# Joint attention with split f32r scores, halved value sums and split keys and queries in place

## The reference

```python
SEQ, CTX, A_HEADS, A_NOPE, A_ROPE, A_V, A_QK = 512, 256, 8, 64, 32, 64, 96
def _attend(q, k, v):
    s = jnp.einsum('bqhd,bkhd->bhqk', q, k).astype(jnp.float32) * (A_QK ** -0.5)
    p = jax.nn.softmax(s, axis=-1).astype(v.dtype)
    return jnp.einsum('bhqk,bkhd->bqhd', p, v)
for l in range(DEPTH):                       # two layers
    fy, gy, qy, ky, vy, ay = _branches(hy, *params, None)      # context, 256 tokens
    fx, gx, qx, kx, vx, ax = _branches(hx, *params, rope)      # sequence, 512 tokens
    ox = _blocked_attention(qx, concat(ky, kx), concat(vy, vx)) * silu(ax)
    x = x + gate * (concat([fx, gx, ox]) @ w_out[l])
    if l < DEPTH - 1:                        # layer 0 alone updates the context
        oy = _attend(qy, ky, vy) * silu(ay)
        y = y + gate_c * (concat([fy, gy, oy]) @ w_out[l])
```

## Time and profile before

| | before |
|---|---|
| median of three runs | 2172.76 us (2172.22 to 2173.36) |
| profiled execution | 2174.57 us, of which the span is 2173.2 us |
| PE busy | 2145.1 us, 99% |
| PE's weight loads | 1754.2 us, 81% |
| VectorE busy | 997.2 us, 46% |
| ScalarE busy | 799.3 us, 37% |
| GpSimd busy | 734.5 us, 34% |
| line 2729, scores | 288 matmuls, 114.6 us |
| line 2741, transposes | 416 matmuls, 60.0 us |
| line 2761, values | 832 matmuls, 87.6 us |

### The profile page before, as it was taken

How to read it: one execution, slowest core, us unless ns; L and a number is a source line. 1 busy time by engine, 2 the same in 40 slices (tenths; PEclk the granted TensorE clock), 3 DMA queues, 4 the chain that set the end, 5 groups by cost and what they waited for, 6 DMA issues and landing times.

```text
span 2173.2 us, 30673 instructions
## 1 busy us (share of the span) xinstructions
PE 2145.1 (99%) x12586; PEld 1754.2 (81%) x12586; DVE 997.2 (46%) x1764; ACT 799.3 (37%) x1371; POOL 734.5 (34%) x339
## 2 busy tenths in 40 slices
PE   9999999999999999999999999999999999999999
PEld 8778888888889898888878888887886667886677
DVE  5664555541222333334465555345305673552672
ACT  6445333333333333334443333333225442334531
POOL 3116444455443333333174444443221002232102
PEclk9999999999999999999999999999999999999999
DMA  4103444432322222221034444322110001322002
GB/s 153 40 30 110 145 145 146 144 126 97 107 93 88 82 81 82 78 88 69 35 121 146 145 146 146 135 97 95 59 68 35 1 1 40 110 78 83 1 2 78
DMA packets 57659, 191.53 MB, mean 88 GB/s; under 512 B 8112, under 2 KB 11440, under 8 KB 57264
## 3 DMA queue, kind: packets, MB, share of 16 engines
q1 hardware_dynamic: 46128, 155.82, 20.6%
q10 hardware_dynamic: 11392, 33.75, 4.4%
HBM read 185.35 MB, written 2.10 MB: 86 GB/s over the span
## 4 chain that ended last, share of the span: by engine, by line
PE 88%; DVE 3%; ACT 1%; issue 1%; DVEq 1%; POOL 0%; ACTq 0%; POOLq 0%; DMA 0%
PE ps L180 21%; PE ps L181 21%; PE ps L182 21%; PE ps L2729 4%; PE ps L183 3%; PE ps L185 3%; PE ps L184 3%; PE ps L2761 2%; PE ps L2741 2%; PE ps L1105 2%; PE ps L1139 1%; PE ps L1121 1%; PE ps L2284 0%; PE ps L2250 0%; PE ps L2097 0%
## 5 line engine op out<-in xcount | busy, mean ns | idle before, releaser
L253 POOL TENSOR_TENSOR w_lo<-w_raw,w_hi 128x1024 fp32r<-128x1024 f32 x282 | 682.0, 2419 | 1332.2 <-ACT w_hi L170 1318.0
L170 ACT ACTIVATE w_hi<-w_raw 128x1024 fp32r<-128x1024 f32 x284 | 300.3, 1058 | 539.3 <-DMA w_raw<-in_wstream 539.0
L180 PE MATMUL ps<-h_hi,w_hi 128*128 128x512 f32 x1168 | 464.0, 397 | 2.7 <-DVE w_lo L295 1.8
L182 PE MATMUL ps<-h_hi,w_lo 128*128 128x512 f32 x1168 | 455.0, 390 | 0.0
L181 PE MATMUL ps<-h_lo,w_hi 128*128 128x512 f32 x1168 | 455.0, 390 | 0.0
L180 PEld LDWEIGHTS ps<-h_hi,w_hi 128*128 128x128 f32 x1168 | 219.3, 188 | 50.7 <-DVE w_lo L295 2.0
L182 PEld LDWEIGHTS ps<-h_hi,w_lo 128*128 128x128 f32 x1168 | 219.3, 188 | 46.0
L181 PEld LDWEIGHTS ps<-h_lo,w_hi 128*128 128x128 f32 x1168 | 219.5, 188 | 43.3 <-issue 0.7
L183 PE MATMUL ps<-w_hi,h_hi 128*128 128x256 f32 x416 | 116.6, 280 | 0.0
L185 PE MATMUL ps<-w_hi,h_lo 128*128 128x256 f32 x416 | 115.5, 278 | 0.0
L184 PE MATMUL ps<-w_lo,h_hi 128*128 128x256 f32 x416 | 115.5, 278 | 0.0
(11 more groups left out here) (362 smaller groups left out, 4019.5 us busy)
## 6 DMA issues: line engine op xcount, KB each, us to landing
w_raw<-in_wstream SPq DMA_DIRECT2D x283, 512.0 KB, 3.2
f0mod_rows<-in_wmod ACTq DMA_DIRECT2D x24, 512.0 KB, 4.6
f1mod_rows<-in_wmod ACTq DMA_DIRECT2D x24, 512.0 KB, 4.6
dvS<-dvE SPq DMA_DIRECT2D x64, 32.0 KB, 2.5
out<-x SPq DMA_DIRECT2D x8, 256.0 KB, 3.2
x<-in_x SPq DMA_DIRECT2D x3, 512.0 KB, 6.9
l_dft<-in_dft ACTq DMA_DIRECT2D x4, 384.0 KB, 4.2
l_wuq<-in_wuq ACTq DMA_DIRECT2D x2, 768.0 KB, 6.1
```

Of the source, the lines that this page charges most:

```text
L170: self.A.activation(self.slot(self.w_hi, n), self.slot(self.w_raw, n), ACT.Copy).then_inc(self.w_high, 1)
L180: T.matmul(out, wh, ah, start=start, stop=False)
L182: return T.matmul(out, wl, ah, start=False, stop=stop)
L253: G.tensor_tensor(c.slot(c.w_lo, n), c.slot(c.w_raw, n), c.slot(c.w_hi, n).bitcast(F32), ALU.subtract).then_inc(c.w_low, 1)
```

## The change

Scores are made as three f32r products. For that keys and queries get a high part and a low part. The low parts lie in place of `kT` and `qT`. The keys' high parts lie in two arrays of four heads where attention's output parts `m_hi[:, 4:8]`, `m_lo[:, 4:8]` lay; these move to `o_hl`, over the used queries. The queries' high parts are a ring of four.

The keys' parts are made in pieces: for heads 0 to 2 the 512 first tokens, one head in each of the steps 6 to 8 of the head jobs, the other tokens of the three in step 9, head 3 as a whole at the first units (high on ScalarE behind exp 0, low on VectorE behind maximum 1), heads 4 to 7 high on ScalarE behind exp 1 to 4 and low on GpSimd. The first four queries are split in two pairs within the head jobs, by ScalarE and VectorE; all later ones by GpSimd during the units, each once the scores four heads before are made.

A pair's value sum is cut: tiles 0 to 2 are summed in step i+3 and tiles 3 to 5 in step i+4, and both come behind the transposes in PE's queue. Gates, spreads and what follows move back by a step for such pairs. In layer 0 scores 0 wait for the second last job's evacuation instead of the last one's, and scores 1 come behind the last transposes.

```diff
@@ class Layer @@
-        self.work = [at(f"work{i}", [P, A_HEADS, A_QK], (ub, ub + ALLT * 4, ua + 4096)[i]) for i in range(3)]
+        self.k_hi = [at(f"k_hi{i}", [A_QK, 4, ALLT], (ua, ub)[i], F32R) for i in range(2)]
...
+        self.k_lo = at("k_lo", [A_QK, A_HEADS, ALLT], c.offset - 2 * A_HEADS * ALLT * 4, F32R)
+        self.q_lo = at("q_lo", [A_QK, A_HEADS, ALLT], c.offset - A_HEADS * ALLT * 4, F32R)
+        self.o_hl = at("o_hl", [P, A_HEADS, ALLT], c.offset - A_HEADS * ALLT * 4, F32R)
@@ tensor_heads @@
             if i == self.nj + 1:
                 if self.turn_bank(self.nj - 1) == self.job_bank(self.nj - 1):
                     T.wait_ge(e.copied_out.h, self.co0 + self.nj - 2)
+                    self.joint.scores(0)
+                    self.joint.scores(1)
                 else:
-                    T.wait_ge(e.evacuated.h, self.ev0 + self.nj)
-                self.joint.scores(0)
-                self.joint.scores(1)
+                    T.wait_ge(e.evacuated.h, self.ev0 + self.nj - 1)
+                    self.joint.scores(0)
...
+        if self.turn_bank(self.nj - 1) != self.job_bank(self.nj - 1):
+            self.joint.scores(1)
@@ scalar_heads @@
             if i == self.nj + 1:
                 self.joint.exp(0)
+                self.joint.keys_high(NT, 3, 4, 0, ALLT)
...
+            if NT <= i < NT + 3:
+                self.joint.keys_high(NT - 2, i - NT, i - NT + 1, 0, SEQ)
+            if i == NT + 2:
+                self.joint.queries_high(0)
+            if i == NT + 3:
+                self.joint.keys_high(NT, 0, 3, SEQ, ALLT)
+            if i == self.nj - 1:
+                self.joint.queries_high(1)
@@ vector_heads @@
             self.finish_job(i)
+            if NT <= i < NT + 3:
+                self.joint.keys_low(c.V, e.parts_low, i - NT + 1, i - NT, i - NT + 1, 0, SEQ)
+            if i == NT + 2:
+                self.joint.queries_low(0)
+            if i == NT + 3:
+                self.joint.keys_low(c.V, e.parts_low, 5, 0, 3, SEQ, ALLT)
+            if i == self.nj - 1:
+                self.joint.queries_low(1)
@@ Joint.__init__ @@
+            gate = self.last[b] + (4 if self.units[self.last[b]][2] == 1 else 3)
             norm = step + (1 if step >= n or not self.both else 0)
+            norm = max(norm, gate)
...
+        self.first = 6 if self.both else 4
@@ Joint.tensor @@
-            if 3 <= i < self.n + 3 and i - 3 in self.of_sum:
-                self.sum_values(i - 3)
             if 2 <= i < self.n + 2:
                 self.turn_probs(i - 2)
+            if i - 4 in self.of_sum and self.units[i - 4][2] == 1:
+                self.sum_values(i - 4, NT // 2, NT)
+            if i - 3 in self.of_sum:
+                self.sum_values(i - 3, 0, NT // 2 if self.units[i - 3][2] == 1 else 2)
@@ scores @@
-        T.wait_ge(e.copied_out.h, self.y.co0 + NT + b + 1)
+        last = self.exps[i] - 1
+        if i < 4:
+            T.wait_ge(e.parts_low.h, self.pl0 + max(5, i + 4))
+        else:
+            T.wait_ge(e.queries_split.h, self.qs0 + last - 3 + min(max(last - self.first + 1, 0), 4))
...
-            ins = T.matmul(c.flat(2 * (i % 2), lo, n), self.y.qT[:, head, self.cols(b)],
-                           self.y.kT[:, head, k0:k0 + n], start=True, stop=True)
+            T.matmul(out, q_hi, k_hi, start=True, stop=False)
+            T.matmul(out, q_lo, k_hi, start=False, stop=False)
+            ins = T.matmul(out, q_hi, k_lo, start=False, stop=True)
@@ new in Joint @@
+    def split_query(self, x):
...
+        G.wait_ge(e.copied_out.h, y.co0 + NT + b + 1)
+        G.wait_ge(e.scored.h, self.sc0 + self.heads[x - 4][0] + 1)
+        G.tensor_tensor(hi, raw, c.ones[0:A_QK, :], ALU.mult)
+        G.drain()
+        G.tensor_tensor(y.q_lo[:, head, self.cols(b)], raw, hi.bitcast(F32), ALU.subtract).then_inc(e.queries_split.h, 1)
+
+    def gpsimd(self):
+        for x in range(4, len(self.heads)):
+            head = x - self.first + 4
+            self.split_query(x)
+            if 4 <= head < A_HEADS:
+                self.keys_low(self.c.G, self.e.queries_split, head + 4, head, head + 1, 0, ALLT)
@@ turn_probs @@
-            T.wait_ge(e.copied_out.h, self.y.co0 + self.y.nj)
+            T.wait_ge(e.copied_out.h, self.y.co0 + self.y.nj - 1)
@@ Joint.vector @@
             if i < self.n:
                 self.max(i)
+            if i == 1:
+                self.keys_low(self.c.V, self.e.parts_low, 7, 3, 4, 0, ALLT)
@@ Joint.scalar @@
             if 0 < i < self.n:
                 self.exp(i)
+            if 0 < i <= 4:
+                self.keys_high(NT, 3 + i, 4 + i, 0, ALLT)
```

More of the change, by code:

```diff
@@ L1708, in __init__ @@
         self.wukv = c.rows[:, 0:1024]
-        self.work = [at(f"work{i}", [P, A_HEADS, A_QK], (ub, ub + ALLT * 4, ua + 4096)[i]) for i in range(3)]
+        self.k_hi = [at(f"k_hi{i}", [A_QK, 4, ALLT], (ua, ub)[i], F32R) for i in range(2)]
+        works = [at(f"work{i}", [P, A_HEADS, A_QK], (ub, ub + ALLT * 4, ua + 3 * ALLT * 4)[i]) for i in range(3)]
+        turn = (NT + self.nt + 2) % 3
+        self.work = [works[(i - turn) % 3] for i in range(3)]
         c.offset = stage1
@@ L2653, in __init__ @@
         for step, (b, bank) in self.spreads.items():
+            gate = self.last[b] + (4 if self.units[self.last[b]][2] == 1 else 3)
             norm = step + (1 if step >= n or not self.both else 0)
+            norm = max(norm, gate)
             self.inverts.setdefault(step - 1, []).append(b)
-            self.gates.setdefault(self.last[b] + 3, []).append(b)
+            self.gates.setdefault(gate, []).append(b)
             self.norms.setdefault(norm, []).append((b, bank))
             self.lows.setdefault(norm + 1 + (step < n), []).append(b)
+        self.heads = [(i, b, hd + s) for i, (b, hd, heads) in enumerate(self.units) for s in range(heads)]
+        end = c.nc.alloc_sbuf_tensor_at(L + "q_hi", [P, 2, P], F32R, offset=layer.tables_end + 256)
+        row = c.nc.alloc_sbuf_tensor_at(L + "q_hi_row", [P, 2, P], F32R, offset=c.row_end - 2 * P * 4)
+        self.q_hi2 = [row[0:A_QK, :, :], end[0:A_QK, :, :]]
+        self.first = 6 if self.both else 4
+        self.q_hi = [row[0:A_QK, 0, :], row[0:A_QK, 1, :], end[0:A_QK, 0, :], end[0:A_QK, 1, :]]
         self.prob = [at(f"prob{i}", spare + i * ALLT * 4) for i in range(3)]
@@ L2753, in sum_values @@
                 T.wait_ge(e.gated.h, self.ga0 + self.nth(done[-1]))
-        for k in range(n):
+        for k in range(k0, k1):
             for s in range(2):
```

47 lines of the change are left out of this document (39 added, 8 removed).

## The result

The changed kernel takes 2183.56 us in the median of four runs (2182.74 to 2183.85), the kernel before beside it on the same chip 2173.06 (2172.22 to 2173.64): 10.5 us more, a ratio of 1.0049, interval 1.0034 to 1.0064. It is slower, and outside the range of the prediction (2168 to 2180).

What follows compares the result with a forecast made beforehand. TensorE's own work was taken to set the period, 5.55 us a pair. Layer 0 at -1.9 and layer 1 at +3.4 made +1.5 us, so 2172.76 became 2174.3, with 2168 to 2180 for 8 in 10.

Steps and rivals of the forecast that it cites:

- Scores at 1.16 us: Both attentions: a 768-wide score call falls from 1.30 to 1.16 us, 64 times, 9.0 us gained; bounds 1.05 and 1.20.
- GpSimd's splits: Query split 1.15 us a head, keys 1.9; hidden except in layer 1's units 4 to 7, +1.9 us.
- rival 2: GpSimd becomes the pace: query split 1.4 us, keys 2.4, giving 2179.1; chance 0.2.
- The pieces: Key pieces under the query jobs delay scores 3: +2.5 us in layer 1, +0.5 in layer 0.
- The uncovered chain of the tail: Layer 1's end: gate, norm, high and low part no longer beside the projection, 3.0 us of PE idle.
- The shared port: VectorE's low parts meet GpSimd's rotations, delaying transposes 8: +0.9 us kept in layer 0, +0.2 in layer 1.
- the three signs: Wrong if f32r passes miss 0.23/0.12 us spacing, GpSimd runs over 20% beyond slope, or entries don't delay scores 3.
- Values in halves: Both attentions: halves 2x0.80 for 1.47 us, +0.13 a pair; unit 2.66; layer 1 0.9 less a block, layer 0 -2.5.
- the clock: Dips cost about 1.7 us each: layer 0 -0.8, layer 1's tail +1.3, its old dip partly covered, -1.0.
- The entry: Layer 1's start: pieces +2.5, GpSimd +1.9, port +0.2, clock -1.0, about 2.0 of overlap taken off.
- the tail: Layer 1's end: +3.1 us of waits and +1.3 of clock dip; layer 0's end 0.
- the rivals, 3: Idle gaps of both entries and the tail keep the clock low longer: +0.8+1.0+1.0, 2177.1; chance 0.15.

Runs made afterwards that it cites:

- e4: Changed kernel with both value halves of layer 1's last pair ahead of the begun output projection: 2181.23 us, 1.0037 of the kernel before.
- e10: Changed kernel with layer 1's last two value halves and the last block's spread all ahead of the begun projection: 2178.12 us, 1.0028 of the kernel before.
- e1: Changed kernel with a fourth buffer for turned probabilities in layer 1 alone: 2179.03 us, 1.0031 of the kernel before.
- e2: Changed kernel with value sums whole and in their old place, gates and spreads at their old steps: 2172.64 us, 1.0002 of the kernel before.
- e3: Kernel before with value sums alone halved behind the transposes, gates and spreads a step later: 2186.25 us, 1.0065 of the kernel before.
- e6: Changed kernel with the key pieces under the query jobs cut to 32 columns, scores therefore different: 2179.70 us, 1.0034 of the kernel before.
- e8: Changed kernel with whole values in their old place and VectorE's copy ahead of its maximum: 2197.39 us, 1.0109 of the kernel before.
- e5: Changed kernel without GpSimd's query splits from layer 0's 13th and layer 1's 9th head on, scores therefore different: 2183.61 us.
- e7: Changed kernel with key pieces behind the root on ScalarE and behind the next job's sum on VectorE: 2182.36 us, 1.0041 of the kernel before.
- e12: Changed kernel, whole values, layer 0's pieces behind root and sum, layer 1's first eight units in f32, no pieces under its query jobs: 2170.22 us, 0.9989 of before.
- e9: Changed kernel with whole values in their old place and layer 0's key pieces behind root and sum: 2172.12 us, 1.0000 of the kernel before.

## Why the prediction was wrong

Forecast 2174.3, measured 2183.56: 9.3 us. Against the forecast of +1.5, the traces have +8.2: 6.7 us that are to be placed.

**Right.** Scores at 1.16 us. GpSimd's splits: 0.45 and 0.45 us, keys 1.82, inside the bounds; rival 2 didn't come, and the 1.9 us that I put down for units 4 to 7 of layer 1 came as one wait of 0.6. The pieces: scores 3 of layer 1 came 2.6 us later than before, counted from the first query projection, forecast 2.5; at the same clock (e4, e10) it is 1.8 to 2.0. The uncovered chain of the tail: 3.07 us of idle, forecast 3.0. The shared port: 1.16 to 1.60 us for 0.86. Against the 0.98 us that the Trainium skill's gap for one matmul would give (TensorE: Matmul & The Clock Gate, section Back-to-back issue gap), the measured 1.16 stands. None of the three signs by which I said the prediction would be wrong appeared: all three were about the passes, GpSimd and the entry, none about the halves.

**Wrong, the step Values in halves** (2.4 us in layer 1, 1.9 in layer 0). I took 0.70 from the transposes to what follows, whatever it is, and +0.13 a pair for the cut; a unit of 2.66. It is 0.75 to values and 0.6 to scores. The halved order is 5.43 a pair on PE alone (e1), 0.11 above my figure, and 0.35 above the whole order (e2, e3), where my working had 0.13 between the two. And I wrote that the copy now has "the transposes and a half sum to hide behind", without following what the copy itself waits for. With three buffers it waits for that same half: 0.15 a pair more (e1). Together 5.58 where I had 5.32, and before 5.55. In layer 0 a half block is 13.77 us where I had 13.5, seven times. The earlier trace rows had the values 0.05 us behind the copy; I read it as a wait about to come, and it was, but it would have been 0.31 a pair (e2), less than the 0.35 and 0.15 of the halves that were to remove it.

**Wrong, the clock.** I forecast a dip behind the tail's idle time, 1.3 us; the profiled execution has none, four others do (below). I took half of layer 0's dip away; after's profile kept it, e1 and e10 with the same code there don't have it. I put a dip at 1.7 us; 3.4 us of low clock cost 0.7 to 1.1 in A and B and 1.5 in D.

**The entry**: B is +2.5, forecast 1.6. At the same clock it is +1.7 to +1.8, so most of the difference is that after's clock was low for 6.8 us there instead of 3.4. The key pieces are 1.0 to 1.2 of it (e6).

**Near in sum, wrong in parts, the tail**: D is +4.6, forecast 3.1+1.3. That the sum came near is luck: the dip didn't come, and 1.5 are left that I didn't have, part of them the last values' wait of 1.1 us for a copy, against 0.5 in e10.

**Outside the attentions**: 1.7 us. 0.9 of them are the second stretch of low clock ahead of A. The other 0.9 lie between A and B and stay open: before, e3 and e8 have 203.7 us there, the other kernels 204.0 to 205.2, all at a clock of 1.00, and e8 has the splits too. Open as well are the 2.3 us between the profiled executions and the medians. The mean granted clock was 0.996 in each of after's four executions and 0.998 or 0.999 in the fourteen of the kernel before that ran beside e1, e2, e3 and e5, where the five with 0.999 took 2170.4 to 2171.4 us and the nine with 0.998 2171.8 to 2174.4. So some of the 10.5 us is clock; how much is due to the change's longer gaps wasn't separated.

In sum: 1.5 for layer 0 (1.9 for its half blocks and 0.8 for the dip that stayed, less 1.2 for what lies at the two ends of A, where no trace was read for it), 2.4 for the steady state of layer 1, 0.9 for its entry, 0.2 for its tail and 1.7 outside are the 6.7. Of the rivals, 3 had the clock low for longer; a part of it came (layer 0's dip, layer 1's entry), the tail's not, and it had nothing of the 4.3 us of the halves. None had the halving itself as the loss. Undoing it takes away all of the measured difference (e2): what the passes then win in the steady state pays for the entry.

## What to carry to other kernels

When a step is cut or moved later, follow what it frees, not only what it hides: a buffer that comes free a step later turns the copy into it into a waiter. Cost the seams between different kinds of PE work by their pair (transposes to scores, transposes to values), each from its own row; many small seams can eat a gain that a measured shorter call has made. And a loop through one bank (scores, maximum, exponential, scores) has to be followed round before an engine's queue is reordered, however idle that engine is.

## What the runs showed of the hardware

The same idle time gave different clocks. In after, e1, e3, e5, e6 and e7 PE stands for 3.07 us at the same place of layer 1's tail. Its first pass behind it took 0.47 us in after and e3, and 0.76 or 0.77 in the four others. The row of e5, and the windows behind it, of after and then of e5 (the last but two numbers are the granted clock):

```profile
2139.30 0.77 PE L181 MATMUL ps<-l_o_hl,w_hi 128*128 128x512 f32 x1 [3.07 <-DVE l_o_hl L2943]
```

```profile
2140.30:2145.30 5.00, 5.00 (x23) 4.13 (x24) 0.75 (x1) 0.00 (x0) 2.39 (x1) 1.00 0.18 67
```

```profile
2139.30:2144.30 5.00, 5.00 (x12) 3.94 (x13) 0.00 (x0) 0.07 (x1) 2.37 (x1) 0.50 0.00 0
```

12 records in 5 us against 23. D was 60.5 us in after, 62.0 in e7, and 63.3 in e5 and e6. So a gap of this size is not 3.07 us but 3.07 plus 0 to 2.8, and one profile doesn't show which; where the gap wasn't there (before, e2, e8 to e12) the clock was 1.00 in each profile.

At layer 1's entry it is the same: behind 3.26 or 3.27 us of idle PE the clock was low for 6.8 us in after and e9, for 3.4 in e1, e2, e4, e5 and e10, and not at all in e8. The windows, of after and then of e8:

```profile
2032.50:2039.30 6.80, 6.18 (x23) 5.53 (x24) 3.73 (x5) 3.89 (x6) 4.53 (x7) 0.50 0.00 0
```

```profile
2035.90:2046.00 10.10, 6.26 (x40) 5.16 (x40) 7.52 (x11) 8.06 (x12) 6.70 (x10) 1.00 0.00 0
```

And at layer 0's entry, behind 1.58 us, it was low for 3.4 or 3.5 us in after, e4 and e8, and not in e1, e2 and e10; behind 1.79 us it was low in the kernel before and not in e3.
